# Layer A of a fused block: first group in order of time with two key chunks, others by residue, softmax joined by shares

## The chip, the cores and the metric

One core of a Trainium2 chip runs the whole program. The metric is the device time of one execution in microseconds (us); lower is better. The engines are TensorE (PE for matmuls, PEld for the weight loads that overlap them), VectorE (DVE), ScalarE (ACT), GpSimd (POOL) and SyncE (SP), which here only issues DMAs.

## What is computed

The program runs three layers over one sequence of 512 tokens of width 1024. Only the first, layer A, is touched. It is a dilated sliding-window attention with 16 heads of 64 features and three groups with dilations 1, 4 and 16:

```python
DILATED_PAIRS = ((128, 1), (512, 4), (2048, 16))
def mixer_a(hn, w_in, w_out, q_gain, k_gain, t5_bias):
    proj = hn @ w_in            # per group q, k, v of width 1024; then a gate of width 1024
    for g, (window, dilation) in enumerate(DILATED_PAIRS):
        q = rms_norm(qkv[:, :, g, 0], q_gain[g])
        k = rms_norm(qkv[:, :, g, 1], k_gain[g])
        v = qkv[:, :, g, 2]
        reach = (window // 2) // dilation          # 64, 64 and 64
        o, lse = dilated_group_attention(q, k, v, t5_bias[...], dilation, reach)
    alpha = jax.nn.softmax(jnp.stack(lses), axis=0)
    y = jnp.sum(alpha[..., None] * jnp.stack(outs), axis=0)
    y = y.reshape(b, s, BRANCH_WIDTH) * jax.nn.silu(gate)
    return y @ w_out
```

The reach is 64 steps of the dilation for all three groups. Merging the groups by their denominators is the same as one softmax over the keys of all groups. In group 0 a query sees the keys at most 64 tokens away; in the other groups only keys of its own residue modulo 4 or 16.

## The kernel before

Sequence positions are held in the order of their residue modulo 4: the 512 columns of every activation are four runs of 128, one for each residue. Eight pairs of heads (128 features each) are worked one after the other. For each pair `attention_layer` projects 11 units: six of queries and keys (u = 0 to 5), the gate (u = 6) and four units of values (u = 7 to 10). A unit of the first seven is 24 matmuls with 512 columns, three split products for each of eight slices of the contraction (`split_product`, L318 to L320: low times high, high times low, high times high of float32 values split in two). A unit of values is 24 matmuls with 384 columns (128 for each of the three groups), with the activations as the stationary operand.

Four attention steps per pair follow, one for each residue of the queries. A step is `scores` (L591: two heads, 768 keys each: the whole sequence for group 0 and one chunk for each other group), `soft_peak` on DVE (L1006: adds the bias and finds the peak), the exponential on ACT (L790), its normalisation on DVE (L1016, L1023), `turn` (L612: six transposes of 128x128 per head), the copies of what was turned (L819 on ACT, L1035 on DVE) and `apply_v` (L629: 12 matmuls), at last `keep_y` (L1043). The steps of a pair are woven by hand between the units of the next pair, in the same order on every engine: `turn` and `apply_v` run one step behind `scores`, so the softmax of a step has a whole step's time. `take` on DVE (L966, L969) moves a query or key unit out of its PSUM bank; it needs 1/norm, for which PE sums the squares in the middle of the next unit (L543, L544), and ACT takes Ln and Exp (L750, L752). In steady running two banks alternate, so unit u may start only when unit u-2 is taken.

Weights come through SP (L519, 512 KB each) into two raw buffers, ACT makes the high part (L733), POOL the low part (L899), in a ring of three slots; a slot's next block is converted when the unit that used it is done. The bias tables of a head come in one DMA on ACT's queue (L725). In the last pair there is no next pair to project; the places between the steps then hold the first two blocks of the output projection, 6 matmuls for each of the eight slices (`early_out`), each slice after its `y_high` (L800 on ACT) and its low part (L938 on POOL). The six other output blocks follow, with the residual add (L1119 on DVE).

Of the kernel before, what the change touches and what calls it, by code (L numbers as in the profile page):

```python
# [1124 lines left out]
def layer_a(T, I):  # L1125
# [3 lines left out]
    L.name, L.index, L.groups = "a", 0, 3  # L1129
    L.w_in, L.w_out = "a_w_in", "a_w_out"  # L1130
    L.x, L.y, L.x_out = T.X0, T.Y, T.Y
    L.raw, L.v_after, L.turn_v = 2, [1, 3, 5], False
    L.score_banks, L.bank_per_head = 3, False
# [3 lines left out]
    L.gain_src = [((lambda g: I["a_q_gain"][0, g].rearrange("(d o) -> d o", o=1)) if t == 0 else  # L1137
                   (lambda g: I["a_k_gain"][0, g].rearrange("(d o) -> d o", o=1)), g)
                  for g in range(3) for t in range(2)]
    L.at = [0, 0, 1, 2, 3, 3, 4, 5, 6, 6, 7]  # L1140
    L.masked = False
    L.squares_at = [(2, 5), (3, 3), (4, 2), (5, 1), (6, 1), (6, 6)]
    L.head_banks = [0, 1, 2, 3, 4, 0, 1, 2, 3, 1, 0]
    L.bias_cols, L.max_cols = A_BIAS, 768
    L.bias_heads, L.bias_at = 3, 3
    L.score_plan = [[(0, 0, 0, 0, 0, 256, False), (1, 2, 256, 1, r * P, P, False), (1, 2, 384, 2, r * P, P, False),
                     (0, 0, 256, 0, 256, 256, False), (1, 1, 0, 0, 0, 256, False), (0, 2, 0, 1, r * P, P, False),
                     (0, 2, P, 2, r * P, P, True), (1, 1, 256, 0, 256, 256, True)] for r in range(4)]
    L.bias_plan = [[((0, 1), (0, 0), 512, 0, (3 - r) * P), ((2, 2), (0, 256), 256, 512, 7 * P)] for r in range(4)]
    L.act_chunks = lambda h, n: 4  # L1150
    L.turn_at = lambda h, c: (c // 4, c % 4 * P)
    L.o_at = lambda t: (1, 256 + t % 2 * P)
    L.chunks = [[(c, 0) for c in range(4)] + [(r, 1), (r, 2)] for r in range(4)]
    L.bias_ap = lambda h: bass.AP(tensor=I["scr_a"].tensor, offset=h * A_ROWS * REL,
                                  ap=[[1, P], [REL, A_ROWS], [1, P]])

    def reorder(out, psum, x):

        o = out.rearrange("p (j c r) -> p c r j", j=16, c=4, r=8)
        v = lambda a: a.rearrange("p (c r j) -> p c r j", c=4, r=8, j=16)  # L1160
        return o, v(psum), v(x)
    L.reorder = reorder
    return L


# [1692 lines left out]
```

## Time and profile before

| | us |
|---|---|
| median of 3 runs (1671.15 to 1674.27) | 1672.38 |
| the profiled execution, whole | 1674.71 |
| its span | 1672.9 |
| PE busy | 1568.7 (94%) |
| PEld busy | 1271.6 (76%) |
| DVE / ACT / POOL busy | 755.5 / 775.8 / 788.4 |
| mean granted TensorE clock | 0.978 |
| attention steps of layer A, from the first scores to the start of the last pair's | 96.66 to 632.09 |

PE is the engine that is nearly always busy; a matmul's end is modelled, so busy time says that work was queued, and how fast PE goes is read from the distance between starts. The three other engines are busy less than half of the span.

### The profile page before, as it was taken

Reading aid. Unit: us, or ns where it says so; the run is one execution under the profiler, and the core shown is the slowest. Engines: PE = TensorE matmul, PEld = TensorE weight load, DVE = VectorE, ACT = ScalarE, POOL = GpSimd, SP = SyncE. Lnnn points to the kernel's source line nnn. Section 1 sums busy time; section 2 is a strip of 40 time slices with the busy share of each in tenths; the row PEclk is TensorE's granted clock in tenths of the full one; section 3 lists DMA queues with packets and bytes.
Section 4 is the critical chain, followed back from the end, with each engine's and each line's share of the span. In section 5 each row is a group of like instructions: output and inputs, shape, how many; then the busy total and the mean of one; then the engine's idle time right before and its main releaser. Section 6 shows DMA issues by size and latency. Waiting matters only on the chain. (4 is left out here: it accounts for less than half of the span.)

```text
span 1672.9 us, 29914 instructions
## 1 busy us (share of the span) xinstructions
PE 1568.7 (94%) x11850; PEld 1271.6 (76%) x11850; DVE 755.5 (45%) x1630; ACT 775.8 (46%) x1436; POOL 788.4 (47%) x475
## 2 busy tenths in 40 slices
PE   6899999999999998989999998998968999899997
PEld 4788888888888886767777776676757887678876
DVE  4224342434434345334454334189436764265535
ACT  4534536363635444346656643245764343352222
POOL 4734425261624342456555543325647652375551
PEclk9999999999999999989999998999988999999999
DMA  7423232232323230254554213432000001333331
GB/s 180 120 59 94 71 96 80 76 101 67 101 70 104 74 90 1 63 149 139 143 154 134 76 51 88 115 70 63 26 28 3 4 3 28 88 89 101 90 92 57
DMA packets 247185, 135.44 MB, mean 81 GB/s; under 512 B 24390, under 2 KB 241518, under 8 KB 246999
## 3 DMA queue, kind: packets, MB, share of 16 engines
q1 hardware_dynamic: 220824, 109.12, 23.5%
q10 hardware_dynamic: 26224, 24.42, 5.2%
q8 instruction: 95, 1.56, 0.4%
q14 instruction: 42, 0.34, 0.1%
HBM read 131.00 MB, written 2.52 MB: 80 GB/s over the span
## 5 line engine op out<-in xcount | busy, mean ns | idle before, releaser
L919 POOL TENSOR_TENSOR a_sq_low<-a_sq,a_sq_high 128x512 fp32r<-128x512 f32 x48 | 62.1, 1293 | 278.4 <-ACT a_sq_high L766 278.4
L318 PE MATMUL a_proj<-h_low,w_high 128*128 128x512 f32 x472 | 190.0, 402 | 1.6 <-POOL h_low L938 0.8
L899 POOL TENSOR_TENSOR w_low<-a_w_raw,w_high 128x1024 fp32r<-128x1024 f32 x64 | 158.5, 2477 | 65.8 <-ACT w_high L733 65.8
L320 PE MATMUL a_proj<-h_high,w_high 128*128 128x512 f32 x472 | 185.7, 393 | 0.0
L319 PE MATMUL a_proj<-h_high,w_low 128*128 128x512 f32 x472 | 184.8, 392 | 0.0
L899 POOL TENSOR_TENSOR w_low<-b_w_raw,w_high 128x1024 fp32r<-128x1024 f32 x40 | 100.4, 2512 | 97.1 <-ACT w_high L733 97.1
L318 PE MATMUL b_proj<-h_low,w_high 128*128 128x512 f32 x288 | 116.5, 405 | 1.4 <-POOL h_low L938 0.8
L320 PE MATMUL b_proj<-h_high,w_high 128*128 128x512 f32 x288 | 113.5, 394 | 0.0
L319 PE MATMUL b_proj<-h_high,w_low 128*128 128x512 f32 x288 | 113.2, 393 | 0.0
L819 ACT ACTIVATE a_pt<-a_turned 128x512 f32<-128x512 f32 x64 | 37.8, 591 | 155.8 <-PE a_turned L612 155.8
L318 PEld LDWEIGHTS a_proj<-h_low,w_high 128*128 128x128 f32 x472 | 88.8, 188 | 23.4 <-DVE a_qk L969 3.2
L320 PEld LDWEIGHTS a_proj<-h_high,w_high 128*128 128x128 f32 x472 | 88.7, 188 | 20.2
L319 PEld LDWEIGHTS a_proj<-h_high,w_low 128*128 128x128 f32 x472 | 88.8, 188 | 18.1
L733 ACT ACTIVATE w_high<-a_w_raw 128x1024 fp32r<-128x1024 f32 x64 | 67.2, 1050 | 38.6 <-PE a_proj L320 17.4
L318 PE MATMUL a_proj<-a_wv_low,h_high 128*128 128x384 f32 x240 | 82.4, 343 | 0.0
L320 PE MATMUL a_proj<-a_wv_high,h_high 128*128 128x384 f32 x240 | 80.6, 336 | 0.0
L319 PE MATMUL a_proj<-a_wv_high,h_low 128*128 128x384 f32 x240 | 80.6, 336 | 0.0
L2688 POOL TENSOR_TENSOR merge_w_low<-f_wt,merge_w_high 128x1024 fp32r<-128x1024 f32 x23 | 56.1, 2441 | 39.3 <-ACT merge_w_high L2634 39.3
L966 DVE SCALAR_TENSOR_TENSOR a_qk<-a_proj,a_gains,a_rn 128x512 f32<-128x512 f32 x22 | 16.5, 751 | 118.2 <-ACT a_rn L752 118.2
L790 ACT ACTIVATE a_probs<-a_logits,a_peak 128x768 f32<-128x768 f32 x64 | 59.7, 933 | 21.5 <-DVE a_peak L1006 20.4
L1686 POOL TENSOR_TENSOR w_low<-sparse_w_raw,w_high 128x1024 fp32r<-128x1024 f32 x15 | 35.9, 2394 | 66.0 <-ACT w_high L1605 61.4
L318 PEld LDWEIGHTS b_proj<-h_low,w_high 128*128 128x128 f32 x288 | 54.4, 189 | 13.5 <-issue 1.6
(488 smaller groups left out, 4202.2 us busy)
## 6 DMA issues: line engine op xcount, KB each, us to landing
a_w_raw<-in_a_w_in_dram SPq DMA_DIRECT2D x78, 512.0 KB, 3.7
b_w_raw<-in_b_w_in_dram SPq DMA_DIRECT2D x30, 512.0 KB, 4.1
b_ada_w<-in_ada_w_dram ACTq DMA_DIRECT2D x24, 512.0 KB, 3.7
f_wt<-in_w_in_dram SPq DMA_DIRECT2D x19, 512.0 KB, 3.8
a_bias<-scr_a ACTq DMA_DIRECT2D x16, 576.0 KB, 4.7
sparse_w_raw<-in_w_in_dram SPq DMA_DIRECT2D x17, 512.0 KB, 3.8
a_w_raw<-in_a_w_out_dram SPq DMA_DIRECT2D x8, 512.0 KB, 3.6
b_w_raw<-in_b_w_out_dram SPq DMA_DIRECT2D x8, 512.0 KB, 3.6
```

Of the source, the lines that this page charges most:

```text
L318: nc.tensor.matmul(out, lh, rl, start=first, stop=False)
L319: nc.tensor.matmul(out, ll, rh, start=False, stop=False)
L320: return nc.tensor.matmul(out, lh, rh, start=False, stop=last)
L733: nc.scalar.activation(high(slot_of(b)), raw[:, n % RAW, :, :], ACT.Copy).then_inc(s_wh, 1)
L790: nc.scalar.activation(into[:, h, 0:n], logits[:, h, 0:n], ACT.Exp, scale=-1.0, bias=col(peak, 2 * h + 1), accum_out=col(total, h)).then_i ...
L819: nc.scalar.activation(pt[:, h, 0:n, :], ps_pt[:, bank, c0:c0 + n * P].rearrange("p (c n) -> p c n", n=P), ACT.Copy).then_inc(s_pa, 1)
L899: nc.gpsimd.tensor_tensor(low(slot_of(b)), raw[:, n % RAW, :, :], high(slot_of(b)), ALU.subtract).then_inc(s_wl, 1)
L919: nc.gpsimd.tensor_tensor(sql[:, :], sq[:, u % 2, :], sqh[:, :], ALU.subtract).then_inc(s_sql, 1)
L966: nc.vector.scalar_tensor_tensor(out=out, in0=v(src), scalar=col(gains, u), in1=v(rn[:, :]), op0=ALU.mult, op1=ALU.mult).then_inc(s_pf, 1)
L1686: nc.gpsimd.tensor_tensor(wl[:, slot(u), :, :], wraw[:, u % RAW, :, :], wh[:, slot(u), :, :], ALU.subtract).then_inc(s_wl, 1)
L2688: nc.gpsimd.tensor_tensor(low(b)[:, :, :], ring.at(b), high(b)[:, :, :], ALU.subtract).then_inc(s_wl, 1)
```

## The change

A function of its own, `dilated_attention`, takes layer A over (`attention_layer` stays for layer B).

- Group 0 is held in order of time. Its queries go into tiles of 128 neighbouring tokens, its keys into chunks of 128 moved by 16 columns (`ROLL`), so that a tile needs two key chunks where it needed four. The groups with dilations 4 and 16 stay by residue, one chunk each. A step so has four chunks, 512 scores per head, where it had six.
- Since the value tiles of group 0 must be in the new order, its values are projected feature by feature, as an eighth unit of 24 matmuls with 512 columns (V0, u = 7), copied into that order (`vfm`) and turned by four transposes (VT, u = 12). The four value units (u = 8 to 11) then have 256 columns instead of 384. A pair has 13 units.
- The tokens of a time tile and of a residue tile differ, so each half of a step (`part` 0 and 1) is exponentiated by its own peak, with its own sum. `swap` copies the 32-row pieces of peaks and sums across (8 small copies per step), `shares` joins them after the fourth step (a chain of eight small instructions with one exponential on ACT), and `normal` then multiplies each half by its share.
- So the four `scores` of a pair come first, with their `soft_peak`, `exps` and `swap`, and all `turn` and `apply_v` after the shares (`PERIOD`, and `LAST` for the last pair).
- The output of a pair collects in one bank (`ps_o`) and is kept once.
- The bias tables of a head come in 17 DMAs on SP's queue: 16 pieces of 32 partitions and one of the rest.
- The gate's sigmoid is made by three ACT functions; a 512-wide reciprocal on DVE goes.

```diff
+    NQK, GATE, V0, VT = 6, 6, 7, 12
+    UNITS, NR, VB, RAW = 13, 8, 2, 2
+    PERIOD = [("S", 0), ("u", 0), ("S", 1), ("u", 1), ("S", 2), ("u", 2), ("S", 3), ("u", 3), ("u", 4),
+              ("T", 0), ("u", 5), ("A", 0), ("T", 1), ("u", 6), ("A", 1), ("T", 2), ("u", 7), ("A", 2), ("T", 3), ("u", 8),
+              ("u", 9), ("A", 3), ("u", 10), ("u", 11), ("u", 12)]
+    LAST = [("S", 0), ("e", 0), ("S", 1), ("e", 1), ("S", 2), ("e", 2), ("S", 3), ("e", 3), ("e", 4), ("e", 5),
+            ("T", 0), ("e", 6), ("A", 0), ("T", 1), ("A", 1), ("T", 2), ("A", 2), ("T", 3), ("A", 3), ("e", 7)]
...
+            def load_bias(head):
+                h = head % 2
+                if head >= 2:
+                    sp.wait_ge(s_l2, 8 * (head // 2 - 1) + 7 + h)
...
+                        sp.dma_start(dst, bass.AP(tensor=I["scr_a"].tensor, offset=at(c, x0 + j0),
+                                                  ap=[[1, 32], [REL, 4], [1, j1 - j0]])).then_inc(s_bias[h], 16)
+                sp.dma_start(bias[:, h, 4 * P:], bass.AP(tensor=I["scr_a"].tensor, offset=at(7, 0),
+                                                         ap=[[1, P], [REL, 2], [1, P]])).then_inc(s_bias[h], 16)
...
+            bias_after = {place["ring", NR * p + 6 + RING]: p for p in range(1, PAIRS)}
...
+            def scores(p, t):
+
...
+                for n in range(4):
+                    for h in range(2):
+                        hp = slice(h * HD, (h + 1) * HD)
+                        g, k0 = (0, 32 * ((t + n) % 4)) if n < 2 else (n - 1, t * P)
...
+            def exps(p, t):
+
+                for h in range(2):
+                    act.wait_ge(s_l2, 2 * (4 * p + t) + h + 1)
+                    for part in range(2):
...
+            def weights(p):
+
+                act.wait_ge(s_chain, CHAIN * p + 3)
+                nc.scalar.activation(diff[:, :, :], diff[:, :, :], ACT.Exp).then_inc(s_ew, 1)
...
+            def swap(p, t):
+
+                dve.wait_ge(s_exp, 4 * (4 * p + t + 1))
+                for b in range(4):
...
+            def shares(p):
+
+                dve.wait_ge(s_swap, 32 * (p + 1))
...
+                for kind, i in plan(p):
+                    if kind == "S":
+                        soft_peak(p, i)
+                        swap(p, i)
+                        if i == 3:
+                            shares(p)
+                            normal(p, 0)
+                    elif kind == "u" and i:
+                        take(p + 1, i - 1)
```

How the instructions stand. On DVE in a middle pair, before, between the soft peak of one step and that of the next (names: `a_qk` is what `take` writes, `a_probs` the probabilities, `a_pt` the turned ones):

```order
L1006 ISA a_logits,a_peak<-a_scores,a_bias 128x512
L1006 ISA a_peak 128x1
L1006 ISA a_logits,a_peak<-a_scores,a_bias,a_peak 128x256
L1035 COPY a_pt<-a_turned 128x256
L966 SCALAR_TENSOR_TENSOR a_qk<-a_proj,a_gains,a_rn 128x4x128
L1016 RECIPROCAL a_inv<-a_total 128x1
L1023 TENSOR_SCALAR a_probs<-a_probs,a_inv 128x768
```

And after, at the fourth step of a pair, up to the take of unit 2:

```order
L1673 COPY a_stat<-a_stat 32x4
L1674 COPY a_stat<-a_stat 32x4
L1681 TENSOR_TENSOR a_lead<-a_stat 128x16
L1684 TENSOR_TENSOR a_diff<-a_lead,a_stat 128x16 x2
L1686 TENSOR_TENSOR a_lead<-a_diff,a_stat 128x16
L1687 TENSOR_TENSOR a_stat<-a_diff,a_stat 128x16
L1689 TENSOR_TENSOR a_lead<-a_lead,a_stat 128x16
L1691 RECIPROCAL a_lead<-a_lead 128x16
L1693 TENSOR_TENSOR a_share<-a_diff,a_lead 128x16
L1702 TENSOR_SCALAR a_probs<-a_probs,a_share 128x256 x4
L1618 SCALAR_TENSOR_TENSOR a_qk<-a_proj,a_gains,a_rn 128x4x128
```

The take (L1618, which was L966) now stands behind the whole chain of the shares and the first normalisation.

On SP at the start of layer A, before and after:

```order
L526 DMA a_gains<-in_a_q_gain_dram 64x1
L526 DMA a_gains<-in_a_k_gain_dram 64x1
L519 DMA a_w_raw<-in_a_w_in_dram 128x8x128 x75
L519 DMA a_w_raw<-in_a_w_out_dram 128x8x128 x2
L519 DMA a_w_raw<-in_b_w_in_dram 128x8x128 x2
```

```order
L1314 DMA a_gains<-in_a_k_gain_dram 64x1
L1303 DMA a_bias<-scr_a 32x4x16 x4
L1303 DMA a_bias<-scr_a 32x4x32 x8
L1305 DMA a_bias<-scr_a 128x2x128
L1293 DMA a_w_raw<-in_a_w_in_dram 128x8x128 x18
```

The 17 bias DMAs stand twice (one set for each head) between the gains and the first weight block of the loop, and again after every tenth weight block.

On ACT in the last pair (`h_high` is what `y_high` writes), before:

```order
L819 ACTIVATE a_pt<-a_turned 128x512
L790 ACTIVATE a_probs,a_total<-a_logits,a_peak 128x768
L800 ACTIVATE h_high<-Y 128x512
L819 ACTIVATE a_pt<-a_turned 128x512 x2
L733 ACTIVATE w_high<-a_w_raw 128x1024
```

And after, on ACT and then on PE:

```order
L1509 ACTIVATE a_probs,a_stat<-a_probs,a_stat 128x256 x4
L1529 ACTIVATE h_high<-Y 128x512
L1515 ACTIVATE a_diff<-a_diff 128x32
L1529 ACTIVATE h_high<-Y 128x512 x3
L1523 ACTIVATE a_pt<-a_turned 128x512
```

```order
L1383 MATMUL a_scores<-a_qk 128x128 x8
L318 MATMUL a_proj<-h_low,w_high 128x512
L319 MATMUL a_proj<-h_high,w_low 128x512
L320 MATMUL a_proj<-h_high,w_high 128x512
L1398 MATMUL a_turned<-consts,a_probs 128x128 x8
L1414 MATMUL a_o<-a_pt,a_v 64x4x32 x4
L1414 MATMUL a_o<-a_pt,a_v 64x128 x4
```

Before, a `y_high` was issued two places ahead of the matmuls that need it, and two slices' matmuls stood in each step; after, `y_high(k)` stands behind the four exponentials of step k, and its six matmuls stand right after that step's scores.

## Rows read from the trace of the kernel before

**Rows 1.** Stretch, length, busy us (count) of PE, PEld, DVE, ACT, POOL; last three: clock, DMA

```profile
260.00:310.00 50.00, 49.97 (x320) 41.43 (x319) 21.13 (x47) 30.02 (x47) 28.68 (x15) 1.00 0.37 106
```

**Rows 2.** Instructions in order of time on PE: start, duration, line

```profile
96.66 1.67 PE L591 MATMUL a_scores<-a_qk 64*128 64x256 f32 x16
...
170.91 1.67 PE L591 MATMUL a_scores<-a_qk 64*128 64x256 f32 x16
172.51 0.87 PE L612 MATMUL a_turned<-consts,a_probs 128*128 128x128 f32 x6
173.14 0.47 PE L318 MATMUL a_proj<-h_low,w_high 128*128 128x512 f32 x1
...
191.68 1.53 PE L629 MATMUL a_turned<-a_pt,a_v 128*64 128x128 f32 x24
193.14 1.67 PE L591 MATMUL a_scores<-a_qk 64*128 64x256 f32 x16
...
247.81 1.67 PE L591 MATMUL a_scores<-a_qk 64*128 64x256 f32 x16
```

**Rows 3.** Projection alone (512, then 384 columns); weight loads before one-column matmuls

```profile
98.60:106.00 7.40, 7.40 (x34) 6.07 (x33) 2.08 (x8) 2.93 (x5) 0.59 (x1) 1.00 0.00 1
84.00:96.00 12.00, 12.00 (x70) 12.00 (x69) 1.68 (x3) 0.00 (x0) 0.00 (x0) 1.00 0.08 23
...
967.16 1.42 PEld L659 LDWEIGHTS b_mod<-consts,b_ada_sum 128*128 128x128 f32 x12
```

**Rows 4.** Small and 256-wide instructions on DVE and ACT, in order of time

```profile
975.92 0.42 DVE L1006 CUSTOM_DVE_ANT_0 b_logits<-b_scores,b_bias 128x256 f32<-128x256 f32 x1 [0.42 <-PE b_scores L591]
...
976.27 0.42 DVE L1006 CUSTOM_DVE_ANT_0 b_logits<-b_scores,b_bias 128x256 f32<-128x256 f32 x1
...
976.48 0.50 ACT L790 ACTIVATE b_raw_probs<-b_logits,b_peak 128x256 f32<-128x256 f32 x1
...
40.94 0.28 DVE L953 TENSOR_SCALAR a_gains<-a_gains 128x1 f32<-128x1 f32 x3 [4.52 <-DMA a_gains<-in_a_k_gain_dram]
```

**Rows 5.** From the summed squares to the take, ACT then DVE, in a middle pair

```profile
182.37 0.69 ACT L750 ACTIVATE a_rn<-a_ss,eps 128x512 f32<-128x512 f32 x1 [1.25 <-PE a_ss L544]
...
183.76 0.75 DVE L966 SCALAR_TENSOR_TENSOR a_qk<-a_proj,a_gains,a_rn 128x512 f32<-128x512 f32 x1 [8.44 <-ACT a_rn L752]
```

**Rows 6.** The first pair: SP's issues, a landing time of the page, conversions, PE

```profile
35.35 0.60 SPq L526 DMA_DIRECT2D a_gains<-in_a_k_gain_dram  x1
38.71 0.37 SPq L519 DMA_DIRECT2D a_w_raw<-in_a_w_in_dram  x1
...
1485.50 0.51 SPq L1223 DMA_DIRECT2D f_wt<-in_w_pb_dram  x1
...
a_w_raw<-in_a_w_in_dram SPq DMA_DIRECT2D x78, 512.0 KB, 3.7
...
47.60 1.05 ACT L733 ACTIVATE w_high<-a_w_raw 128x1024 fp32r<-128x1024 f32 x1
...
49.04 2.41 POOL L899 TENSOR_TENSOR w_low<-a_w_raw,w_high 128x1024 fp32r<-128x1024 f32 x1
...
49.70 0.39 PE L318 MATMUL a_scores<-h_low,w_high 128*128 128x512 f32 x1
...
77.20 0.66 PE L318 MATMUL a_scores<-a_wv_low,h_high 128*128 128x384 f32 x1 [3.60 <-POOL a_wv_low L899]
```

**Rows 7.** The last pair, and a stretch of another layer in which PE mostly waits

```profile
632.09 1.67 PE L591 MATMUL a_scores<-a_qk 64*128 64x256 f32 x16
...
635.99 0.61 ACT L800 ACTIVATE h_high<-Y 128x512 fp32r<-128x512 f32 x1
...
636.68 1.67 POOL L938 TENSOR_TENSOR h_low<-Y,h_high 128x512 fp32r<-128x512 f32 x1 [23.75 <-ACT h_high L800]
...
674.13 1.08 DVE L1119 TENSOR_TENSOR Y<-a_proj,X 128x512 f32<-128x512 f32 x1 [3.08 <-PE a_proj L320]
...
1245.00:1250.00 5.00, 1.70 (x2) 0.12 (x1) 4.96 (x6) 2.18 (x4) 2.04 (x2) 0.50 0.24 71
```

More of the change, by code:

```diff
@@ L1122, in _, with layer_a_space @@
             add_square(nc, dve, T, sq, s_nsq, s_acc, KT - 1)
-def layer_a(T, I):
+def layer_a_space(T, I):
     L = Space()
[L1129 to L1133, printed above, removed]
+    L.w_in, L.x, L.index = "a_w_in", T.X0, 0
     width = HEADS * HD
@@ L1136, in layer_a @@
                              else ((i - 7) * 3 + 2) * width) + p * P
[L1137 to L1161, printed above, removed]
@@ L2809, in build @@
         T.causal = part("causal")
-        a, b = layer_a(T, I), layer_b(T, I)
+        a, b = layer_a_space(T, I), layer_b(T, I)
         w_in = I["w_in_2"][0].rearrange("(k p) n -> p k n", p=P)
@@ L2816, in build @@
         retire(nc, T)
-        attention_layer(nc, T, I, a)
+        dilated_attention(nc, T, I, a)
         retire(nc, T)
```

494 lines of the change are left out of this document (493 added, 1 removed).

## The prediction

> **What bounds the kernel now.** I first read the busy time by stretch: in the middle of layer A PE is busy 49.97 of 50 us at full clock, the other engines at most 30 [rows 1]. Then PE in order of time. The first step of a pair starts at 170.91 and 247.81, so a pair costs 76.9 us, and all of it is PE issue: what PE does not issue is gained, and every new wait is lost. Two places of layer A are not like that. In the first pair PE waits for weights (3.6 us at 77.20 [rows 6]), and in the last pair there is little to put between the steps: from its first scores (632.09) to the end of the two early output blocks, which DVE takes at 674.13, are 42.0 us [rows 7]. I cost the change in these three places. Layers after A are untouched. The sum is made against the profiled execution (1674.71 us, span 1672.9) and then laid on the median of the runs, 1672.4, 2.3 below it.
>
> **Part 1: what PE issues in a pair.** Of a stretch of n matmuls the pitch is (length + one duration) / n: (7.40 + 0.39) / 34 = 0.229 us at 512 columns and (12.00 + 0.34) / 70 = 0.176 at 384 [rows 3]. 128 columns less are 0.053 less, so 256 columns should be 0.123. The bounds: no gain at all (0.176), and the weight load alone, 12 in 1.42 us or 0.118 [rows 3]. I take 0.123, on the line of the two measured points.
> - V0: 24 matmuls more at 0.229, +5.5.
> - Value units: 96 matmuls from 0.176 to 0.123, -5.1.
> - Scores: a step takes 1.60 (170.91 to 172.51 [rows 2]) for 1536 columns, in future 1024. If all of it scaled it would be 1.07; with some fixed start I take 1.15. Four steps: -1.8.
> - Transposes: six take 0.63 (172.51 to 173.14 [rows 2]), so 0.1 each; 48 become 32, and four for VT: -1.2.
> - Values times probabilities: 12 matmuls take 1.46 (191.68 to 193.14 [rows 2]), 0.12 each; 48 become 32: -2.0.
> - One more change between kinds of matmul (nine groups after, eight before), at the 0.1 to 0.25 that such a seam costs: +0.2.
> Sum -4.4 us a pair, 72.5 for 76.9. The strided keys and outputs (four runs of 32) have no row; I take them at nothing, and would see up to half a us a pair.
>
> The Trainium skill (TensorE: Matmul & The Clock Gate, Back-to-back issue gap) gives an isolated gap of N/2.4 + 2.5 ns, 109 ns at 256 columns; by it the value units would save 1.3 us a pair more, 11 in all. It would also give 216 ns at 512 columns, where the trace has 229 [rows 3]; the measurement decides.
>
> **Part 2: a new wait in each of seven pairs.** Unit u needs unit u-2 taken. Unit 4 starts 24 matmuls and two for the squares after the fourth scores: 26 x 0.229 = 6.0 us. The take of unit 2 now stands on DVE behind soft peak, swap, shares and the first normalisation of that step. From the end of these scores: ACT is busy until 2.0 with squares and two conversions of unit 2 (two of 0.6, two of 1.05); the soft peak of the first head is done at 0.8 (pitch 0.35 of a 256-wide one [rows 4]), so the four exponentials, 0.5 each [rows 4], end at 4.1. Eight swaps: three independent small instructions take 0.28, so a pitch of 0.07 [rows 4], 0.6 in all: 4.8. Then minimum, two differences, the exponential on ACT, two products, sum, reciprocal, product: seven waits at about 0.2 to 0.25 each (0.15 for the smallest instruction [rows 4] and the signal), 1.7: 6.5. Four multiplications of 256 at 0.25: 7.5. Ln and Exp of unit 2, on ACT behind the shares' exponential, are done at 7.0 (1.39 from the start of Ln to the take [rows 5]), so DVE is last; the take of 0.75 [rows 5] ends at 8.3. PE waits 8.3 - 6.0 = 2.3 us. Bounds: 1 with a chain of 0.15 a link, 4 with 0.3 a link and swaps of 0.15. So a pair costs 74.8, not 72.5. The other takes have one us or more to spare by the same count.
>
> **Part 3: SP's queue.** 34 bias DMAs now stand between two weight loads. Back to back an issue holds SP 0.37 (a weight block alone), 0.51 (after another) or 0.60 (a gain, 64 rows) [rows 6]; I take 0.5 with the gap, 17 us a pair. In the middle: the block before them goes out 7.4 us after unit 4 ends: squares 1.3 on ACT, their low part 1.3 and two low parts of 2.4 [rows 6] on POOL. The block behind them goes out at 25 and lands 3.7 later [rows 6]. ACT meets it in order, after unit 7 and before the copy of the fourth turned tile, which the last `apply_v` needs at 30.2 (units 5 and 6 at 6.0, unit 7 at 5.5, two value units 6.0, four turns and three applications 6.8). 7.9 + 17.0 + 3.8 + 1.05 for the high part + 0.75 for the copy = 30.5: a wait of 0.3. At 0.37 there is none, at 0.64 it is 5. So I add 0.3 a pair: 75.1, and 7 x 75.1 = 525.4 from the first scores to those of the last pair. Before it was 632.09 - 96.66 = 535.4 [rows 2, 7]. **-10.0**.
>
> **Part 4: the first pair.** The gains end on SP at 36.0, and the first weight block of the loop went at 38.71 [rows 6]. Now 34 x 0.5 stand there: it goes at 53.0 (49 to 58) and lands at 56.7; 1.05 on ACT and 2.4 on POOL [rows 6] make it ready at 60.2. It is for unit 4, which PE could start at 49.70 + 12 x 0.229 = 52.4 [rows 6]. That is 7.8 us of waiting (4 to 13), and some 2.5 for half clock behind it and 2 for squares that come late on ACT behind the same block. Against it: the 3.6 us at 77.20 [rows 6] and the 2.5 of half clock behind them go, since value blocks are needed one unit later. The units themselves: +5.5 for V0, -5.1, +0.6 for VT. 7.8 + 2.5 + 2 - 3.6 - 2.5 + 1.0 = 7.2, less some 2.8 that squares and weights wait before 77.20 now and would not, then: first scores at 101.1 for 96.66 [rows 2], **+4.4** (-1 to +10).
>
> **Part 5: the last pair.** Before, a step held two slices' matmuls, and their `y_high` was done earlier. Now scores, soft peak, four exponentials, `y_high`, low part and six matmuls are one chain: 1.15 + 0.13 + 0.7 + 2.0 + 0.6 + 1.5 + 0.2 for signals, then 1.5 = 7.8 us (durations from [rows 4, 7]), of which PE works 2.6. Three such steps: 23.3. The fourth adds swap and the first shares, 1.4, before its `y_high`: slice 3 starts at 31.0; slices 3 to 5 and a turn: 36.2. Copy, `y_high`, low part, slice 6: 40.4. Four `apply_v` and three `turn`, each behind a copy of 0.7: 49.1. `keep_y` 0.8, `y_high` 0.6, low part 1.6, slice 7 1.4: 53.5 at full clock. In another layer, where PE is busy 1.7 of 5 us, the granted clock is 0.50 [rows 7], the 1.2 GHz level. With PE at a third here I expect that for most of the first 35 us: up to 0.85 more for each of four scores and 1.4 for each of six slices, 11.8; I take 9. 62.5 for 42.0: **+20.5** (+11 to +25). The same page of the Trainium skill (Part 1: The HAM clock gate) says that idle gaps let the clock gate halve the clock until PE is busy again; by that rule the half clock is there, and the trace agrees with it in the stretch of rows 7.
>
> **Off the path:** the reciprocal that goes from DVE (3.4 us a pair) and the two ACT functions in its place, the smaller softmax, and one `keep_y` a pair: these engines have slack in the middle [rows 1].
>
> **Sum:** +4.4 - 10.0 + 20.5 = +14.9. 1672.4 + 14.9 = **1687**.
>
> **The rivals.**
> - *The matmuls that went decide.* The chain of the shares is short enough (1 us of wait), unit 4 of the first pair waits 3 us, and the clock stays up in the last pair: 7 x 73.5 = 514.5 is 20.9 less, and -1 - 20.9 + 11.5 = -10.4, 1662; without any wait in the middle 7 x 72.5 gives -28 and with the head at -3 the end is -19.5, 1653. For it: PE is the only bound in the middle [rows 1]. Against: the last pair's chain is made of measured durations. Faster than before; it decides where the take of unit 2 comes within 6.5 us of the fourth scores.
> - *SP's queue is worse than I took it.* At 0.64 an issue the last `apply_v` of seven pairs waits 5 us, and the first pair's unit 4 waits 13: 7 x 4.7 + 6.5 = +39 more, 1725. For it: the gains' pitch is just that [rows 6]. Against: they are of another shape, and weight blocks take 0.37.
> - *256 columns cost what 384 do,* since the weight load does not hide: 8 x 5.1 = +41, 1727. Against: the weight load alone needs 0.118 [rows 3].
>
> **How the numbers follow.** The forecast with its bounds (the share wait 1 to 4, the head -1 to +10, the last pair +11 to +25) spans 1674 to 1701: 0.66. Matmul saving decides: 0.16 (1650 to 1671). SP's queue 0.08, of which a half beyond 1706; wide value units 0.05; in between 0.05. The range 1668 to 1706 leaves out some 0.1 below and 0.1 above. 0.2%, 3.3 us, is about what a measurement of this kernel can tell from no change. Faster by more than that 0.15, within it 0.09, slower 0.76.
>
> **What would show it.** In the profile after: a period of 74 to 76 us between first scores; a wait of PE before unit 4 of each pair, released by the take (`a_qk`) on DVE; a first gap of PE of some 6 us near 52; six PE gaps of 4 to 5 us in the last pair with the clock at 0.5, and 55 to 65 us from its first scores to the end of slice 7. A period under 73 would take away part 2; a period over 78 would point to SP or to the value units, whose pitch the trace shows directly.

## The result, and where the time stands in the profile after

The changed kernel takes 1738.7 us (median of 4 runs, 1737.5 to 1745.8) against 1672.2 for the kernel before on the same chip: ratio 1.0405, 95% interval 1.0375 to 1.0435. Slower, as forecast, but by 66 us and not by 15. The profiled execution has a span of 1744.0 us for 1672.9. It is the slowest of its four: of the 71.1 us between the spans, 64.1 lie in the three places below, 2.3 ahead of layer A and 4.7 behind the early output blocks of its last pair.

I read the same three places as before the change. First PE in order of time: the first scores of the first pair, of three neighbouring pairs in the middle, and of the last (start, duration, engine, line). They answer to [rows 2, 7].

```profile
103.84 1.16 PE L1383 MATMUL a_scores<-a_qk 64*128 64x128 f32 x16
...
186.07 1.16 PE L1383 MATMUL a_scores<-a_qk 64*128 64x128 f32 x16
...
267.48 1.16 PE L1383 MATMUL a_scores<-a_qk 64*128 64x128 f32 x16
...
349.97 1.16 PE L1383 MATMUL a_scores<-a_qk 64*128 64x128 f32 x16
...
677.33 1.16 PE L1383 MATMUL a_scores<-a_qk 64*128 64x128 f32 x16
```

The seven periods take 573.5 us, 81.9 each; before they took 535.4, 76.5 each with the first. The forecast was 75.1. The two other places, with the wait before unit 4 of the first pair, and then the first and the fourth of the waits for a slice in the last pair:

```profile
64.19 0.79 PE L318 MATMUL a_turned<-h_low,w_high 128*128 128x512 f32 x1 [8.80 <-POOL w_low L1574]
...
683.63 0.76 PE L318 MATMUL a_proj<-h_low,w_high 128*128 128x512 f32 x1 [5.14 <-POOL h_low L1593]
...
714.28 0.80 PE L318 MATMUL a_proj<-h_low,w_high 128*128 128x512 f32 x1 [6.79 <-POOL h_low L1593]
```

- First pair: layer A's first matmul is at 30.01 (27.68 before), so its first scores come 73.8 us later, against 69.0 before: +4.8. The 2.3 us ahead of it are no effect of the change: in the runs below the layer's first matmul lies between 27.0 and 30.7.
- Last pair: from its first scores to the early output blocks, which DVE takes at 740.52, are 63.2 us against 42.0 [rows 7]: +21.2.

So the ends came as forecast (+4.4, +20.5), and the whole miss is in the middle: +38.1 us where -10.0 were expected. The middle in two windows, the first with the wait before unit 4 behind it (columns as in [rows 1], the last three are granted clock, DMA share, GB/s):

```profile
260.00:310.00 50.00, 44.95 (x262) 36.71 (x263) 22.02 (x92) 23.25 (x55) 19.28 (x10) 0.93 0.22 64
...
546.83:552.18 5.35, 5.29 (x13) 4.13 (x13) 0.01 (x1) 0.50 (x1) 3.23 (x2) 0.50 0.13 38
...
580.10:585.70 5.60, 5.60 (x50) 5.60 (x49) 1.84 (x5) 0.00 (x0) 0.00 (x0) 1.00 0.61 150
```

PE is busy 44.95 of 50 us for 49.97 [rows 1]. The last row is two value units of 256 columns: (5.60 + 0.28) / 50 = 0.118 us a matmul, even under the 0.123 forecast. The row above it is the first half of unit 4 at a granted clock of 0.50. What PE waits for, from its timeline in one pair:

```profile
541.83 0.40 PE L320 MATMUL a_proj<-h_high,w_high 128*128 128x512 f32 x1
546.89 0.80 PE L318 MATMUL a_proj<-h_low,w_high 128*128 128x512 f32 x1 [4.67 <-DVE a_qk L1618]
547.49 0.63 PE L319 MATMUL a_proj<-h_high,w_low 128*128 128x512 f32 x1
...
588.16 0.44 PE L1414 MATMUL a_o<-a_pt,a_v 128*64 128x128 f32 x4 [2.13 <-ACT a_pt L1523]
```

The wait before unit 4 is the forecast one, released by the take on DVE, and it is 4.67 or 4.68 us in all seven pairs, where 2.3 were expected. Behind it 24 matmuls, the wait among them, take 12.88 us where 5.71 would do: 2.5 us more go to the half clock. The wait at the last `apply_v` is 1.66 to 2.71 us instead of 0.3. Now DVE, in order of time from ACT's last exponential of the fourth step:

```profile
540.14 2.23 DVE L1673 COPY a_stat<-a_stat 32x4 f32<-32x4 f32 x1 [2.47 <-ACT a_probs L1509]
542.30 0.15 DVE L1674 COPY a_stat<-a_stat 32x4 f32<-32x4 f32 x1
542.48 0.16 DVE L1673 COPY a_stat<-a_stat 32x4 f32<-32x4 f32 x1
...
543.27 0.18 DVE L1681 TENSOR_TENSOR a_lead<-a_stat 128x16 f32<-128x16 f32 x1
...
545.04 1.14 DVE L1702 TENSOR_SCALAR a_probs<-a_probs,a_share 128x256 f32<-128x256 f32 x4
546.09 0.75 DVE L1618 SCALAR_TENSOR_TENSOR a_qk<-a_proj,a_gains,a_rn 128x512 f32<-128x512 f32 x1
```

and POOL in the same stretch:

```profile
537.58 2.42 POOL L1574 TENSOR_TENSOR w_low<-a_w_raw,w_high 128x1024 fp32r<-128x1024 f32 x1
539.94 2.42 POOL L1574 TENSOR_TENSOR a_wv_low<-a_w_raw,a_wv_high 128x1024 fp32r<-128x1024 f32 x1
```

Four elements on 32 partitions take 2.23 us, and the seven copies like it 0.15 or 0.16. The long one ends at 542.37, POOL's low part at 542.36. In all seven pairs this copy takes 2.23 or 2.24 us, and it is not the only one. Of the 256 copies of the swaps 24 take over 0.3 us (0.81 to 2.24); each of them ends within 0.03 us of the end of an instruction of POOL, and they are all the copies that began while POOL still had more than 0.2 us to go. The experiments below ask whether POOL causes it.

### The profile page after: what moved, and what is told of

It is laid out like the page before. It is cut to its first block and busy times, and to the rows that moved or that the text cites. A ratio compares the mean times of both kernels' runs of the same rounds, so it can differ in the third digit from the quotient of the medians.

```text
span 1744.0 us, 30166 instructions
## 1 busy us (share of the span) xinstructions
PE 1561.0 (90%) x11690; PEld 1249.5 (72%) x11690; DVE 771.6 (44%) x1942; ACT 770.7 (44%) x1556; POOL 786.2 (45%) x479
## 5 line engine op out<-in xcount | busy, mean ns | idle before, releaser
L318 PE MATMUL a_proj<-h_low,w_high 128*128 128x512 f32 x520 | 221.2, 425 | 59.6 <-DVE a_qk L1618 32.7
L1574 POOL TENSOR_TENSOR w_low<-a_w_raw,w_high 128x1024 fp32r<-128x1024 f32 x72 | 177.4, 2464 | 160.9 <-ACT w_high L1468 160.9
L320 PE MATMUL a_proj<-h_high,w_high 128*128 128x512 f32 x520 | 214.4, 412 | 0.0
L319 PE MATMUL a_proj<-h_high,w_low 128*128 128x512 f32 x520 | 213.2, 410 | 0.0
L1509 ACT ACTIVATE a_probs<-a_probs,a_stat 128x256 f32<-128x256 f32 x128 | 63.2, 495 | 99.6 <-DVE a_stat L1665 99.6
L1618 DVE SCALAR_TENSOR_TENSOR a_qk<-a_proj,a_gains,a_rn 128x128 f32<-128x128 f32 (+2 forms) x76 | 37.0, 522 | 130.4 <-ACT a_rn L1478 130.0
L1673 DVE COPY a_stat<-a_stat 32x4 f32<-32x4 f32 x128 | 44.5, 347 | 58.2 <-ACT a_probs L1509 55.2
L318 PE MATMUL a_proj<-a_wv_low,h_high 128*128 128x256 f32 x240 | 68.2, 284 | 0.0
L320 PE MATMUL a_proj<-a_wv_high,h_high 128*128 128x256 f32 x240 | 66.9, 279 | 0.0
L319 PE MATMUL a_proj<-a_wv_high,h_low 128*128 128x256 f32 x240 | 66.8, 279 | 0.0
```

The costliest lines, as they stand in the source:

```text
L318: nc.tensor.matmul(out, lh, rl, start=first, stop=False)
L319: nc.tensor.matmul(out, ll, rh, start=False, stop=False)
L320: return nc.tensor.matmul(out, lh, rh, start=False, stop=last)
L1509: nc.scalar.activation(e, e, ACT.Exp, scale=-1.0, bias=stat[:, own, part, t, h, 0:1], accum_out=stat[:, own, part, t, h, 1:2]).then_inc(s_ ...
L1574: nc.gpsimd.tensor_tensor(low(slot_of(b)), raw[:, n % RAW, :, :], high(slot_of(b)), ALU.subtract).then_inc(s_wl, 1)
L1618: return nc.vector.scalar_tensor_tensor(out=out, in0=x, scalar=col(gains, u), in1=r, op0=ALU.mult, op1=ALU.mult)
```

## The experiments

All are the changed kernel with the edit shown. The edits are shown in short: conditions on the pair, helper functions and semaphore increments are left out. A wait or a duration "per pair" is read from PE's timeline in the seven pairs. The ratios are to the kernel before, which ran beside each group of experiments (medians 1673.2 to 1675.2 us); "less" in us is the difference of the medians from the changed kernel's 1738.7.

### The take of unit 2 ahead of the shares

```diff
 ACT, step 3:    exps(p, i)
+                inv_norm(p + 1, 2)
                 weights(p)
-    "u" 3:      inv_norm(p + 1, 2)
 DVE, step 3:    soft_peak(p, i)
+                take(p + 1, 2)
                 swap(p, i)
                 shares(p); normal(p, 0)
-    "u" 3:      take(p + 1, 2)
```

> The changed kernel, in which only the take of unit 2 of the next pair (and the Ln and Exp that it needs on ACT) stands ahead of swap, shares and normalisation at the fourth step of seven pairs. Theory: PE's wait before unit 4 (4.68 us in the changed kernel) is the take's place in DVE's order, and the half clock in the 24 matmuls behind it is its consequence. Then the wait is 0 to 0.4 us, those matmuls take 5.7 instead of 8.2 us, and a pair costs 7.2 us less: 1739 - 50 = 1689 (ratio to the kernel before 1.010). Rival A: the clock falls there for a reason of its own; then only the 4.7 go and the time is 1706. Rival B: the first turn of the step then waits for shares and normalisation, which come 0.8 us later; at most 1 us a pair comes back, 1696, seen as a wait of PE before the turn.

Measured: 1708.2 us, ratio 1.0206 (1.0183 to 1.0229), 30 us less: a smaller gain than the theory's 50, and also than that of either rival (1706 and 1696). The number is near rival A's, but the trace speaks against it: the wait before unit 4 is 0.13 us, and no half clock follows. The gain is partly given back at a place that none of the three had named, on PE's timeline:

```profile
593.99 0.50 PE L1334 MATMUL a_ss<-a_sq_low,pair_ones_r 128*128 128x512 f32 x1 [1.35 <-POOL a_sq_low L1590]
```

ACT waits with `weights` for the differences (2.43 us), and the square of unit 3 stands behind it. Also, in two of the seven pairs the two value units behind the wait at the last `apply_v` took 7.0 to 7.1 us where 5.5 would do. And DVE's timeline shows the same event at another operation, the four instructions of the first normalisation, while POOL works from 592.64 to 596.34 (DVE, then POOL):

```profile
592.45 4.30 DVE L1704 TENSOR_SCALAR a_probs<-a_probs,a_share 128x256 f32<-128x256 f32 x4
...
592.64 1.29 POOL L1590 TENSOR_TENSOR a_sq_low<-a_sq,a_sq_high 128x512 fp32r<-128x512 f32 x1 [2.88 <-ACT a_sq_high L1492]
593.89 2.45 POOL L1576 TENSOR_TENSOR w_low<-a_w_raw,w_high 128x1024 fp32r<-128x1024 f32 x1
```

### The square of unit 3 ahead of the shares too

```diff
 ACT, step 3:    inv_norm(p + 1, 2)
+                square(p + 1, 3)
                 weights(p)
-    "u" 3:      square(p + 1, 3)
```

> As the run with the early take, and on ACT the square of unit 3 (and its high part) stands ahead of the shares' exponential too. Theory: what the early take left, 1.35 us of PE's wait for the low part of that square in each pair, comes from ACT, which holds the square back while it waits for the shares' differences. Then this wait goes and the time is 1708 - 9 = 1699, or a few us less if the normalisation is not held. Rival: the low part on POOL now starts 1.5 us earlier, and the shares and the normalisation of the first slice, which work from SBUF to SBUF on DVE, stand still behind it and behind the weight's low part (3.7 us); then PE waits 1 to 2.5 us before the first turn instead, and the time is 1704 to 1712.

Measured: 1689.3 us, ratio 1.0094 (1.0071 to 1.0117): 19 us less than without it, more than the 9 expected. No wait for the squares is left in the middle; 0.8 us a pair have come at the first `apply_v` (the hold on DVE, the rival's sign at a smaller size), and the wait at the last `apply_v` fell from 2.0 to 0.7 us on average, probably because the low parts on POOL, and the weight blocks on SP that wait for them, start earlier; no run tries this apart. The two edits together give back 49 of the 66 us.

### What holds the copy: another form of it, and POOL out of its way

```diff
-nc.vector.tensor_copy(stat[into, other, 1, 3 - b, :, :], stat[rows, own, 0, t, :, :])
+nc.vector.tensor_reduce(stat[into, other, 1, 3 - b, :, :],
+                        stat[rows, own, 0, t, :, :].rearrange("p h (s o) -> p h s o", o=1),
+                        axis=mybir.AxisListType.X, op=ALU.max)
```

> The changed kernel, in which only the form of the eight small moves of a swap is another (a reduction over one element instead of a copy); order and data are the same. In the changed kernel the first copy of the fourth step takes 2.24 us and ends with POOL's low part of a value block, the other seven 0.15 each. Theory: the SBUF-to-SBUF copy waits until POOL's instruction is done, and the reduction does not. Then the first move takes 0.15 to 0.2 us, PE's wait before unit 4 falls from 4.7 to 2.6 us, 15 us in seven pairs, 1724; and up to 1706 if the shorter wait leaves the clock up. Rival: the first small instruction behind ACT's accumulated sums is slow whatever it is (or waits for ACT's write); then nothing moves, 1739.

Measured: 1731.2 us, ratio 1.0344 (1.0328 to 1.0359), 7 us less. DVE and POOL in one pair:

```profile
530.59 0.14 DVE L1673 TENSOR_REDUCE a_stat<-a_stat 32x4 f32<-32x4 f32 x1 [2.46 <-ACT a_probs L1509]
530.67 0.13 DVE L1674 TENSOR_REDUCE a_stat<-a_stat 32x4 f32<-32x4 f32 x1
...
531.56 1.28 DVE L1681 TENSOR_TENSOR a_lead<-a_stat 128x16 f32<-128x16 f32 x1
...
530.40 2.41 POOL L1574 TENSOR_TENSOR a_wv_low<-a_w_raw,a_wv_high 128x1024 fp32r<-128x1024 f32 x1
```

The first move takes 0.14 us, so the rival (slow behind ACT's sums, whatever it is) falls. In the whole run 146 of the 256 reductions began with more than 0.2 us of a POOL instruction to go, and none takes more than 0.15 us. But the theory missed half of its own gain: the minimum of the shares, which reads two SBUF operands, now takes 1.28 us for 0.18 and ends at 532.84, POOL's instruction at 532.81. PE's wait is 3.62 us and not 2.6.

The other side of it, less for POOL to do at that moment, and the copies kept:

```diff
-V_AFTER = (2, 4)
+V_AFTER = (3, 4)
```

> The changed kernel, in which only the first value block of each pair is fed one unit later (behind unit 3 instead of unit 2), so that POOL has nothing to do while DVE swaps at the fourth step; the swap's copies and their place are unchanged. Theory: the first copy waits for POOL's instruction, not for ACT's sums. Then it takes 0.15 to 0.3 us instead of 2.24, and no other operation of the share chain takes over the wait, as the first two-input operation did with the reductions; PE's wait before unit 4 falls from 4.68 to 2.6 us and the half clock behind it from 2.5 to 1.5 us or less: 7 x 2.1 to 7 x 3.1 less, 1739 - 18 = 1721. Rival: the copy itself is slow behind the sums (2.2 us whatever POOL does): 1739.

Measured: 1721.1 us, ratio 1.0283 (1.0259 to 1.0307). The wait before unit 4 is 2.32 us in all pairs. POOL, then DVE, in one pair:

```profile
520.95 2.42 POOL L1574 TENSOR_TENSOR w_low<-a_w_raw,w_high 128x1024 fp32r<-128x1024 f32 x1
...
522.57 0.83 DVE L1673 COPY a_stat<-a_stat 32x4 f32<-32x4 f32 x1 [1.52 <-ACT a_probs L1509]
523.32 0.15 DVE L1674 COPY a_stat<-a_stat 32x4 f32<-32x4 f32 x1
...
524.29 0.17 DVE L1681 TENSOR_TENSOR a_lead<-a_stat 128x16 f32<-128x16 f32 x1
```

The copy is not 0.15 to 0.3 but 0.83: with one `w_high` less ahead of them the exponentials end a microsecond earlier, and the copy runs into the weight block's low part, which ends at 523.37. Nothing is held after that. The edit also moves a conversion on ACT, so its 18 us are not the price of the hold alone; what it shows is that the copy's duration follows the end of POOL's instruction when that end moves (2.23, 0.83 and, in the run with the early take, 0.34 us). So it is POOL's running instruction that holds it.

The Trainium skill (SBUF — State Buffer, Who interferes with whom) has this rule: VectorE and GpSimd share one pair of SBUF ports under an exclusive lock; copies and `tensor_scalar` can take it, an operation with two SBUF inputs meets GpSimd's reads, and `tensor_reduce` never contends on trn2. The trace agrees in each of the four cases: copy 2.23 us for 0.15, two-input minimum 1.28 for 0.18, four `tensor_scalar` 4.30 for 1.14, reduction 0.14. The trace of before could have shown it. Its normalisation is of this kind. From the second of the middle pairs on it is never held (instances, then ns least, median and most), but there it meets no more than the last 0.24 us of an instruction of POOL:

```profile
L1023 DVE TENSOR_SCALAR a_probs<-a_probs,a_inv x48: 620/621/660, 184.6 to 628.2; 128x768 f32<-128x768 f32 x48
```

In the pair before those it is held once, 1.13 us for 0.62, while POOL works until 117.64. And in the last pair POOL's low part, begun just behind a normalisation, takes 1.67 us [rows 7], where one that meets none takes 1.27 (each time DVE, then POOL):

```profile
116.93 1.13 DVE L1023 TENSOR_SCALAR a_probs<-a_probs,a_inv 128x768 f32<-128x768 f32 x1
115.25 2.39 POOL L899 TENSOR_TENSOR a_wv_low<-a_w_raw,a_wv_high 128x1024 fp32r<-128x1024 f32 x1
...
636.61 0.62 DVE L1023 TENSOR_SCALAR a_probs<-a_probs,a_inv 128x768 f32<-128x768 f32 x1
671.79 1.27 POOL L938 TENSOR_TENSOR h_low<-Y,h_high 128x512 fp32r<-128x512 f32 x1 [7.97 <-ACT h_high L800]
```

Four of the eight low parts of that pair begin 0.07 to 0.08 us behind a normalisation and take 1.67 to 1.69 us. So the engine that comes second seems to be the one that waits; this direction is read from these rows only, no run tries it.

### The biases on SP, in the middle

```diff
-                if n in bias_after:
-                    for h in range(2):
-                        load_bias(2 * bias_after[n] + h)
+                for h in range(2):
+                    if n - h in bias_after:
+                        load_bias(2 * bias_after[n - h] + h)
```

> The changed kernel, in which only the 17 bias DMAs of the second head of a pair go out one weight block later on SP. Theory: PE's wait of 2.2 us at the last apply_v comes from the weight block that stands behind all 34 on SP, for which ACT waits ahead of its copy of the turned tile. Then that block goes out 8.7 us earlier, ACT does not wait for it, the wait is 0, and seven pairs gain 15 us: 1723. Rival: the next block, now behind the other 17, takes over; PE waits as long at the next pair's first units, 1739. The wait before unit 4 (4.7 us) stays in both.

Measured: 1720.5 us, ratio 1.0286 (1.0269 to 1.0304), 18 us less. No wait at the last `apply_v` is left in any pair, the next block did not take over, and the wait before unit 4 is unchanged at 4.67 us. So this wait was SP's queue. Its terms in the changed kernel, SP and ACT:

```profile
563.68 8.67 SPq L1303 DMA_DIRECT2D a_bias<-scr_a  x16
572.39 0.43 SPq L1305 DMA_DIRECT2D a_bias<-scr_a  x1
572.87 7.77 SPq L1303 DMA_DIRECT2D a_bias<-scr_a  x16
580.69 0.44 SPq L1305 DMA_DIRECT2D a_bias<-scr_a  x1
581.17 9.29 SPq L1293 DMA_DIRECT2D a_w_raw<-in_a_w_in_dram  x3
...
586.57 1.06 ACT L1468 ACTIVATE w_high<-a_w_raw 128x1024 fp32r<-128x1024 f32 x1 [12.32 <-DMA a_w_raw<-in_a_w_in_dram]
```

34 DMAs take 17.5 us (17.0 forecast). The block behind them is there 5.4 us after its issue (when ACT, which waits for it, starts), where I had taken 3.7 to 3.8, close to the median of all weight blocks.

### The biases on SP, in the first pair

```diff
-            for head in range(2):
-                load_bias(head)
 ...
                 load(n)
+                if n - RAW in (4, 6):
+                    load_bias((4, 6).index(n - RAW))
```

> The changed kernel, in which only the 34 bias DMAs of the first pair stand later on SP: one head's behind the seventh weight block of the loop's list, the other's two blocks later, instead of ahead of all of them. Theory: PE's 8.8 us before unit 4 of the first pair are these DMAs ahead of the weight block; then that wait is 0 to 1 us and the first scores start 6 to 9 us earlier, unless a later block takes over: 1739 - 7 = 1732. Rival: the weight blocks between them come too late, and PE waits 3 to 8 us before a value unit or one of the units 6 and 7: 1736 to 1740.

Measured: 1742.8 us, ratio 1.0415 (1.0387 to 1.0444): nothing gained, as the rival says for the time. The wait of 8.8 us before unit 4 is gone, and one of 9.65 us stands at 79.7, not at one of the places that the rival named but before the squares of unit 4, which come late on ACT behind a value block that waits for its DMA:

```profile
79.72 0.80 PE L1334 MATMUL a_ss<-a_sq_low,pair_ones_r 128*128 128x512 f32 x1 [9.65 <-POOL a_sq_low L1588]
```

```diff
-            for head in range(2):
-                load_bias(head)
+            first_bias = (x for head in range(2) for x in bias_dmas(head))
 ...
                 load(n)
+                for _ in range(5):
+                    next(first_bias, None)
```

> The changed kernel, in which only the 34 bias DMAs of the first pair are issued in fives behind the first weight blocks of the loop, instead of all ahead of them. Theory: SP has 3 to 5 us between two weight blocks while it waits for POOL, and five DMAs of 0.5 us fit in there; PE's wait before unit 4 (8.8 us) goes and none takes its place: first scores at 95 to 98 instead of 103.8, 1739 - 7 = 1732. Rival: as with 17 in one piece, which moved the wait to the squares of unit 4 (9.65 us), every later block is 2.6 us later and the sum of the waits in the first pair stays at 8 to 10 us: 1739.

Measured: 1735.0 us, ratio 1.0359 (1.0326 to 1.0392). In the trace the theory holds: the waits over 0.25 us in this pair are 0.27 and 2.87, and the first scores come 63.5 us after the layer's first matmul, where it was 73.8 (and 69.0 before). In the medians 3.6 us of the 10 arrive, by the ratios some 8; the intervals overlap, so the size is not settled by the times.

### The last pair: y_high ahead of the exponentials

```diff
 ACT, last pair, step i:
+                y_high(0), y_high(1)    # i == 0; else y_high(i + 1)
                 exps(p, i)
-                y_high(i)
```

> The changed kernel, in which only the order on ACT in the last pair is another: the copies y_high of the slices stand one to two steps ahead of the exponentials instead of behind those of their step. Theory: the 63 us of the last pair come from the chain scores, soft peak, exponentials, y_high, low part, slice; then the four steps take 11 to 14 us instead of 37, with a remaining chain of swap, shares, turns and applications of 25 to 27 us: 38 to 42 us, 1739 - 22 = 1717. Rival: POOL's low parts (1.6 us) and the half clock set the steps, 5 us each; then 1728.

Measured: 1726.4 us, ratio 1.0307 (1.029 to 1.0325), 12 us less. From the first scores to the last `apply_v` are 41.5 us for 57.6. A step takes 5.1 us for 9.9, so the order on ACT was half of a step. That is the rival's size and not the 2.7 to 3.5 of the theory, but for another reason than the rival's: the next soft peak stands behind the swap, which waits for the exponentials, and one copy of each of three swaps is held by POOL's low part (DVE, second step):

```profile
684.38 0.17 DVE L1676 COPY a_stat<-a_stat 32x4 f32<-32x4 f32 x1
684.46 1.26 DVE L1677 COPY a_stat<-a_stat 32x4 f32<-32x4 f32 x1
...
686.02 0.42 DVE L1666 CUSTOM_DVE_ANT_1 a_probs<-a_scores,a_bias 128x256 f32<-128x256 f32 x1
```

### All together, and one part taken out of it

The early take and square, the reductions, the split of the biases in the middle, the later biases of the first pair in two pieces, `y_high` ahead, and in the last pair on DVE also `soft_peak(p, i + 1)` ahead of `swap(p, i)`:

> The changed kernel with the moves together: take of unit 2 and square of unit 3 ahead of the shares, swap by reductions, the second head's biases one block later, the first pair's biases later, and in the last pair y_high ahead of the exponentials and the next soft peak ahead of the swap. Theory: the losses found are separate and add: -37 (middle, with the square), -18 (bias in the middle), -6 (first pair), -23 (last pair): 1739 - 84 = 1655, below the kernel before (1673, ratio 0.990). Rival: half clock behind the remaining small waits and POOL's hold on DVE's SBUF operations take a part of it, 2 us a pair: 1670, no gain over the kernel before.

Measured: 1653.9 us, ratio to the kernel before 0.9888 (0.985 to 0.9926). The sum is met, but not term by term, and the close agreement is in part luck. In the traces the middle gives 63.8 us where 55 were added up (573.5 to 509.7), the first pair 1.2 for 6 (a wait of 9.6 us stands before the squares of unit 4, as with the later biases alone), and the last pair 21.8 for 23 (63.2 to 41.4). The middle has no PE wait over 0.25 us in seven pairs, and the period is 72.8 us: the matmul count without a wait.

> The five moves together, with the first pair's bias DMAs in fives behind the weight blocks instead of in two pieces of 17. Theory: the middle stays at a period of 72.85 us without waits, and the first pair gains what the 9.6 us of waiting there cost: 1654 - 8 = 1646 (ratio to the kernel before 0.984). Rival: the first pair's wait only moves again: 1654.

Measured (biases of the first pair in fives): 1653.0 us, ratio 0.9872 (0.9848 to 0.9895). The first scores come 65.8 us after the layer's first matmul for 72.6, but in four of the seven pairs the period is now 73.8 to 73.9, with a wait of 0.8 us at the first `apply_v`. So the number is the rival's, but the reason is not: the first pair gained, and the middle gave it back. The wait is behind DVE, which is held twice in the shares (1.16 and 2.42 us for 0.18 and 0.17) and then at length in the second normalisation, behind which the copy of the turned tile stands: its four instructions, 1.14 us where nothing holds them, take 6.50 and end with the third of three instructions of POOL. In the pairs without the wait they end with the second, over 2 us earlier. Little separates the two: in the 28 middle pairs of the four runs with the early take and square, this normalisation begins at most 14.72 us behind the fourth scores where the wait is not there, and at least 14.76 where it is. DVE, then PE:

```profile
491.22 1.16 DVE L1707 TENSOR_TENSOR a_lead<-a_diff,a_stat 128x16 f32<-128x16 f32 x1 [0.29 <-ACT a_diff L1528]
...
492.50 2.42 DVE L1710 TENSOR_TENSOR a_lead<-a_lead,a_stat 128x16 f32<-128x16 f32 x1
...
497.17 6.50 DVE L1723 TENSOR_SCALAR a_probs<-a_probs,a_share 128x256 f32<-128x256 f32 x4
503.59 0.68 DVE L1731 COPY a_pt<-a_turned 128x512 f32<-128x512 f32 x1
...
504.41 0.84 PE L1421 MATMUL a_o<-a_pt,a_v 128*64 128x128 f32 x11 [0.84 <-DVE a_pt L1731]
```

The times cannot tell it from the version before it. Both beat both kernels.

> As six_moves, but the swap by copies as in the changed kernel. Theory: with the take of unit 2 ahead, the swap is off the path of PE in the middle, so POOL's hold on the copies costs nothing there; in the last pair three steps are some 1 us longer. 1646 + 3 = 1649. Rival: the copies delay shares and normalisation behind POOL's low parts, and PE waits 1 to 2 us before the first turn in seven pairs: 1657.

Measured: 1654.9 us, ratio 0.9883 (0.9861 to 0.9905), not to be told from 1653.0. Off PE's path the held copies cost nothing that the times can tell. In the trace the wait of 0.8 us at the first `apply_v` stands in six pairs instead of four (2.4 us more in the middle), but that count went from none to four with no edit in the middle; the rival's wait before the first turn is 0.2 us, not 1 to 2.

> As six_moves, but the take of unit 2 and the square of unit 3 behind the shares as in the changed kernel (the swap by reductions). Theory: the wait before unit 4 is then 3.6 us as in the run with reductions alone, and 1 to 1.7 us of half clock stand behind it, in seven pairs: 1646 + 7 x 5 = 1681. Rival: with the other waits gone the clock stays up, and only the 3.6 us return: 1671.

Measured: 1687.3 us, ratio 1.0077 (1.0058 to 1.0096): 34 us for the place of two instructions in two queues, 4.9 a pair, and 6 us above the theory's 1681. Each pair has the wait of 3.6 us, as both expected. What decides is behind it: 1.6 us go to the half clock in two pairs and 2.8 in the other five (the two matmuls of the squares counted in), so the clock does not stay up, against the rival, and falls for longer than the theory's 1 to 1.7.

## Why the prediction was wrong, step by step

- **Part 1, what PE issues:** right. 0.118 us at 256 columns for 0.123; a score step takes 1.09 (1.15 forecast), eight transposes 0.79 to 0.85, an application 1.02. With the waits taken off, the pair is 78.4 - 4.67 - 1.7 = 72.1 us in the run with split biases, and 72.8 in the combination; 72.5 was forecast. The strided keys cost nothing that shows.
- **Part 2, the wait before unit 4:** right place, right releaser, wrong size, and beyond the upper bound of 4. The exponentials end 4.1 us after the scores, as forecast, and the shares take 1.77 for 1.7. The swap took 3.1 us for 0.6: 2.1 is POOL's hold, the rest a pitch of 0.13 for 0.07. I had priced eight small copies by the rows of three small instructions with an idle POOL [rows 4] and had looked at nothing that runs beside them, though the trace of before had one normalisation held (at 116.93). This is 2.4 us a pair.
- **A term that was not there:** I counted the half clock in the first and the last pair and left it out behind the waits in the middle. It is 2.5 us in the 24 matmuls and 0.3 in the two behind them: 2.8 us a pair, more than the error of the wait itself.
- **Part 3, SP's queue:** the mechanism right, the size 2.3 us for 0.3. Of the 2.0, 1.6 is the landing of the weight block behind 34 small transfers. The margin was a difference of two sums of 30 us, so an error of 5% in one was all of it. The rival of 5 us had the place and the direction; its cause, 0.64 us an issue, was not it: an issue held SP 0.51.
- **Part 4, the first pair:** +4.8 for +4.4, with the wait before unit 4 at 8.8 us for 7.8. The landing behind the small DMAs took 1.9 us more than I had taken here too (ACT starts on the block 5.6 us after its issue), and the wait only 1.0 more: that the sum came so close is in part luck.
- **Part 5, the last pair:** +21.2 for +20.5. The granted clock from 677 to 715 is 0.62, where I had taken a half for most of it, and the four gaps between slices and scores are 5.0 to 6.8 us (the other two that I expected are 2.2 and 2.8). The chain was made of measured durations, and it held. One of them was itself a held one: the 1.5 to 1.6 us for a low part come from a row of 1.67 [rows 7], and it takes 1.26 here. (In the rivals, 1687 + 39 and 1687 + 41 are 1726 and 1728, not 1725 and 1727.)

So the steps that failed are three terms of the middle: the price of the swap, the half clock put at nothing behind the waits, and the landing behind SP's small DMAs. The middle by terms: 2.4 + 2.8 + 2.0 - 0.3 (PE issues 72.2 us a pair for 72.5) = 6.9 us a pair, 48 in seven, which is the miss in the middle (573.5 for 525.4). The rival in which the matmul saving decides described this kernel without its waits: 25.7 us are saved in the middle (509.7 for 535.4) once the waits are out.

## What to carry to other kernels

Price a new instruction by what the neighbouring engine does at that moment, not by its length: where DVE works from SBUF to SBUF beside POOL, add the rest of POOL's instruction, up to its whole length, and again for each further instruction that meets one, or take a form that does not meet it. A hold shows as one long instance of an instruction and not as a wait with a releaser, so look for single instances far above their median. Where a new chain has two engines' queues in it, first ask which unrelated instruction stands behind it in each; here two moves in order were worth 49 us, with no operation saved. A wait of PE of some us is priced with the half clock that can stand behind it, and many small DMAs ahead of a large one by its landing too, not by their issue alone.

## What the runs showed of the hardware

- A DVE copy, a `tensor_scalar` and a two-input operation, all in SBUF, wait for POOL's running instruction; a 16-byte copy on 32 partitions does so as well (2.23 us for 0.15). A reduction does not (0.13 to 0.15 in all 146 instances that met one). POOL's instructions were two-input operations with both inputs in SBUF; no other kind was tried.
- What half clock costs behind a wait varies for the same wait (before unit 4, with the two matmuls of the squares counted in). Behind 4.67 us it was 2.7 to 2.9 us in the changed kernel and 1.6 to 2.5 with split biases; behind 3.6 us, with the reductions alone, 1.5 to 1.7 in six pairs and 0.1 in one, and in the last experiment 1.6 in two pairs and 2.8 in five; behind 2.3 us 0.1 in five pairs and 1.6 to 1.7 in two; behind the 2.2 us at the last `apply_v` 0 to 1.6. What decides between them was not tried.
- A weight block of 512 KB is there 3.7 us after its issue (median before), 5.4 to 5.6 behind 34 transfers of 8 to 128 KB, and 6.4 behind 17 of them in the run with the later first biases (68.51 to 74.89). What lengthens it was not tried apart.
